# Delta-net inverses kept as two 64 x 64 diagonal blocks below the top level

## The reference

```
L = strict_lower((k * beta) @ k.T * decay);  a = L + I
sol = triangular_solve(a, [v * beta, k * beta * exp(gc)])
```

## Time and profile before

| | |
|---|---|
| median of 3 runs (lowest to highest) | 1391.28 us (1390.93 to 1394.15) |
| the profiled execution, its time | 1388.38 us |
| its span, 19281 instructions | 1386.8 us |
| PE busy | 1199.2 us (86%) |
| DVE, POOL, ACT busy | 579.5 (42%), 463.7 (33%), 382.1 (28%) us |
| mean granted TensorE clock | 0.942 of full speed |

### The profile page before, as it was taken

The page is one execution under the profiler, slowest core; times in us unless marked ns, Lnnn a source line. Parts: engine busy times, 40 slices in busy tenths (PEclk is TensorE's granted clock), DMA queues, the critical chain, the costliest instruction groups (busy, mean ns, idle before and its releaser), DMA issues. The chain is left out here.

```text
span 1386.8 us, 19281 instructions
## 1 busy us (share of the span) xinstructions
PE 1199.2 (86%) x7621; PEld 890.2 (64%) x7621; DVE 579.5 (42%) x1182; ACT 382.1 (28%) x796; POOL 463.7 (33%) x464
## 2 busy tenths in 40 slices
PE   5989999699998884999789999789999789998883
PEld 4866788655554442877678887678888745555541
DVE  4456863411111116454775455775474411111113
ACT  4325641011111003354333355333432111111000
POOL 1222001122222211155886166986230022222210
PEclk8999999699999996999999999999999789999997
DMA  7122035779999995021000111000327779999995
GB/s 222 62 67 77 1 124 211 308 290 387 380 390 393 382 378 216 3 82 39 2 1 1 62 61 61 1 1 1 152 78 270 308 285 372 386 391 385 387 369 212
DMA packets 65803, 270.29 MB, mean 195 GB/s; under 512 B 16812, under 2 KB 16908, under 8 KB 41136
## 3 DMA queue, kind: packets, MB, share of 16 engines
q1 hardware_dynamic: 54176, 247.50, 47.0%
q0 software_dynamic: 11392, 21.00, 4.5%
q10 hardware_dynamic: 144, 0.52, 0.1%
HBM read 262.69 MB, written 23.07 MB: 206 GB/s over the span
## 5 line engine op out<-in xcount | busy, mean ns | idle before, releaser
L874 POOL DMA_INDIRECT y_rows<-arena,idx_i x64 | 64.9, 1015 | 366.5 <-DVE arena L1153 359.6
L1489 PE MATMUL bank<-arena 128*128 128x128 f32 x1088 | 139.3, 284 | 17.2 <-DVE arena L2008 8.1
L1489 PEld LDWEIGHTS bank<-arena 128*128 128x128 f32 x1088 | 129.8, 196 | 29.9 <-DVE arena L2008 11.2
L991 PE MATMUL bank<-ring,arena 128*64 128x256 f32 x1024 | 126.2, 398 | 15.0 <-issue 14.0
L1157 DVE TENSOR_TENSOR arena<-arena,bank 128x128 f32<-128x128 f32 x64 | 18.4, 288 | 279.2 <-ACT arena L1068 279.2
L1068 ACT ACTIVATE arena<-bank 128x128 f32<-128x128 f32 x64 | 17.8, 278 | 379.6 <-PE bank L991 241.1
L144 PE MATMUL bank<-ring_r,ht_r 128*128 128x512 f32 x288 | 113.5, 394 | 0.0
L991 PEld LDWEIGHTS bank<-ring,arena 128*64 128x64 f32 x1024 | 76.2, 137 | 54.5 <-issue 16.9
L1153 DVE COPY arena<-bank 128x512 f32<-128x512 f32 x64 | 44.3, 692 | 149.4 <-PE bank L1000 149.4
L142 PE MATMUL bank<-ring_r,arena_r 128*128 128x512 f32 (+1 forms) x228 | 91.3, 400 | 5.4 <-DVE ring_r L166 3.4
L143 PE MATMUL bank<-ring_r,arena_r 128*128 128x512 f32 x224 | 88.3, 394 | 0.0
(11 more groups left out here) (303 smaller groups left out, 2364.3 us busy)
## 6 DMA issues: line engine op xcount, KB each, us to landing
ring<-in_moe_w_gate SPq DMA_DIRECT2D x32, 1024.0 KB
ring<-in_moe_w_up SPq DMA_DIRECT2D x32, 1024.0 KB
ring<-in_moe_w_down SPq DMA_DIRECT2D x26, 1024.0 KB
arena<-in_moe_w_down SPq DMA_DIRECT2D x20, 1024.0 KB
ring<-in_gdn_w_in SPq DMA_DIRECT2D x8, 2048.0 KB, 8.1
arena<-in_moe_w_gate SPq DMA_DIRECT2D x12, 1024.0 KB
arena<-in_moe_w_up SPq DMA_DIRECT2D x12, 1024.0 KB
spare<-in_moe_w_down SPq DMA_DIRECT2D x10, 1024.0 KB
```

Source lines behind the costliest of these rows:

```text
L874: pool.indirect_dma_start(out=y_rows[l], out_offset=bass.IndirectOffsetOnAxis(ap=idx_i[:, 1, e:e + 1], axis=0), in_=y_out[:, e % RING, :], ...
L991: last = pe.matmul(bank[1][m * SLOTS:(m + 1) * SLOTS, 0:2 * P].rearrange("p (w n) -> p w n", w=2), xgt[:, i, c * SLOTS:(c + 1) * SLOTS], w ...
L1489: last = pe.matmul(bank[b][:, h * P:(h + 1) * P], lhs(h), rhs(h), start=True, stop=True)
```

## The change

`level`, `seed` and a new `unit` become 128 x 64 masks: rows 0 to 63 hold the upper left block, rows 64 to 127 the lower right one. Up to level 5 (`TOP = 6`) the tiles `lm`, `w`, `r`, `s` and `st` hold only these two blocks, 4 heads x 64 columns, 256 in all. `sides_act` (ACT, two copies per chunk) cuts the blocks out of `lt`. Each product becomes two, one per block, on rows and columns 0 to 63 or 64 to 127 of the array; the turns become products with the identity. At level 6 `y` reads the two off-diagonal blocks of `lt` directly, and DVE writes the update into the off-diagonal blocks of `s` (two copies per slot). `make_v0`, `diag_pool` and `keep_pool` go: POOL keeps the masks `lm` and gets `top_pool` (two operations per slot, once per pair), ACT gets the copies by `move` and, at level 6, two copies per slot into the diagonal blocks of `s`.

```diff
+        def by_side(pe, b, lhs, rhs, across=False):
+            for h in range(HH):
+                for i, side in enumerate(SIDES):
+                    to = SIDES[1 - i] if across else side
+                    last = pe.matmul(bank[b][to, h * HB:(h + 1) * HB], lhs[side, h, to] if across else lhs[side, h, :],
+                                     rhs[side, h, :], start=True, stop=True)
+            return last
+        def turn_sides(pe, b, src):
+            for h in range(HH):
+                for side in SIDES:
+                    last = pe.matmul(bank[b][side, h * HB:(h + 1) * HB], src[side, h, :], ident[side, side],
+                                     start=True, stop=True)
...
-                    four(pe, 3 * slot, lambda h: lm[slot][:, h, :], lambda h: r_buf[l % 2][slot][:, h, :]
+                    by_side(pe, 3 * slot, lm[slot] if l < TOP else lt_of(2 * p + slot), r_buf[l % 2][slot],
+                            across=l == TOP).then_inc(g["y"], 1)
...
-                        turn_four(pe, 3 * slot + 2, s_buf[slot]).then_inc(g["t"], 1)
+                        turn_sides(pe, 3 * slot + 2, s_low[slot]).then_inc(g["t"], 1)
...
-                    four(pe, 3 * slot + 1, lambda h: st_buf[slot][:, h, :], lambda h: w_buf[slot][:, h, :]
+                    by_side(pe, 3 * slot + 1, st_low[slot], w_low[slot]).then_inc(g["un"], 1)
...
+        def sides_act(act, n):
+            act.wait_ge(g["lt"], n + 1)
+            for side in SIDES:
+                last = act.copy(lt_side_of(n)[side, :, :], lt_of(n)[side, :, side])
+            last.then_inc(g["lt_side"], 1)
...
+            if first:
+                for slot in range(2):
+                    sides_act(act, 2 * p + slot)
...
-                        act.copy(flat(st_buf[slot]), bank[3 * slot + 2][:, :]).then_inc(g["se"], 1)
+                        act.copy(flat(st_low[slot]), bank[3 * slot + 2][:, 0:HH * HB]).then_inc(g["se"], 1)
...
+                if l < TOP:
+                    for slot in range(2):
+                        act.activation(flat(s_low[slot]), flat(r_buf[l % 2][slot]), ACT.Copy,
+                                       scale=move[:, l:l + 1]).then_inc(g["rb"], 1)
+                else:
+                    for slot in range(2):
+                        act.wait_ge(g["top"], 2 * p + slot + 1)
+                        for side in SIDES:
+                            last = act.copy(s_buf[slot][side, :, side], lm[slot][side, :, :])
+                        last.then_inc(g["top_kept"], 1)
...
+        def top_pool(pool, o, p, slot):
+            pool.wait_ge(g["y"], at_level(p, TOP - 1, slot))
+            pool.wait_ge(g["r"], at_level(p, TOP, slot))
+            o.step(pool.tensor_tensor(lm[slot], r_buf[TOP % 2][slot], by_head_side(unit), ALU.subtract))
+            pool.wait_ge(g["sn"], at_level(p, TOP - 1, slot))
+            pool.tensor_tensor(lm[slot], lm[slot], s_low[slot], ALU.add).then_inc(g["top"], 1)
...
-                    pool.tensor_tensor(lm[slot], lt_of(n), by_head(level[l]), ALU.mult).then_inc(g["lm"], 1)
+                    pool.tensor_tensor(lm[slot], lt_side_of(n), by_head_side(level[l]), ALU.mult).then_inc(g["lm"], 1)
...
+        def first_st_r(dve, o, n, b):
+            dve.wait_ge(g["lt_side"], n + 1)
...
+            dve.tensor_tensor(st_low[n % 2], lt_side_of(n), by_head_side(seed), ALU.mult)
+            dve.wait_ge(g["m1"], n + 1)
+            o.step(dve.tensor_tensor(r_odd[n % 2], sides_in(bank[b]), by_head_side(seed), ALU.mult))
+            dve.tensor_tensor(st_low[n % 2], st_low[n % 2], by_head_side(unit), ALU.add)
+            dve.tensor_tensor(r_odd[n % 2], r_odd[n % 2], by_head_side(unit), ALU.add).then_inc(g["r"], 1)
...
+                        for i, side in enumerate(SIDES):
+                            last = dve.tensor_copy(s_buf[slot][side, :, SIDES[1 - i]],
+                                                   sides_in(bank[3 * slot + 1])[side, :, :])
+                        last.then_inc(g["sn"], 1)
```

More of the change, by code:

```diff
@@ L701, in build @@
         DIRS, LEVELS = 2, 7
-        MASKS = LEVELS + 4
+        TOP, HB = LEVELS - 1, P // 2
+        SIDES = (slice(0, HB), slice(HB, P))
+        MASKS = 7
         MASKS_AT = 17408 - MASKS * P
[L704 to L708, removed]
+        side_masks = cut(MASKS_AT, TOP + 2, HB)
+        level = [None] + [side_masks[:, l - 1, :] for l in range(1, TOP)]
+        seed, unit = side_masks[:, TOP - 1, :], side_masks[:, TOP, :]
+        incl = cut(MASKS_AT + 4 * P, DIRS, P)
+        below = cut(MASKS_AT + 6 * P, P)
         differ = cut(0, P)
-        at_least = cut(D, LEVELS + 1, P)
+        differ_s = cut(P, HB)
+        incl_s = cut(2 * P, DIRS, HB)
+        at_least = cut(D, TOP + 1, HB)
         bits = cut(2 * D, 2 * P).bitcast(I32).rearrange("p (w n) -> p w n", w=2)
         odd = cut(2 * D + 2 * P, LEVELS)
-        swap = cut(2 * D + 3 * P, P)
-        lower = cut(3 * D, LEVELS + 1, P)
+        swap = cut(2 * D + 3 * P, HB)
+        lower = cut(3 * D, TOP, HB)
         stay = sb("stay", [P, LEVELS])
@@ L736, in masks_dve @@
             o.step(dve.tensor_copy(differ, bits[:, 0, :]))
[L737 to L740, removed]
+            for side in SIDES:
+                dve.tensor_copy(differ_s[side, :], differ[side, side])
+                dve.tensor_copy(unit[side, :], ident[side, side])
+                for d in range(DIRS):
+                    dve.tensor_copy(incl_s[side, d, :], incl_of(d)[side, side])
@@ L741, in masks_dve @@
+            dve.memset(odd[SIDES[0], TOP:LEVELS], 0.0)
+            o.step(dve.memset(odd[SIDES[1], TOP:LEVELS], 1.0))
+            for l in range(TOP):
+                dve.tensor_scalar(at_least[:, l, :], differ_s, float(2 ** l), None, ALU.is_ge)
+            o.step(dve.memset(at_least[:, TOP, :], 0.0))
+            for l in range(1, TOP):
                 dve.tensor_tensor(level[l], at_least[:, l, :], at_least[:, l + 1, :], ALU.subtract)
             o.step(dve.tensor_tensor(seed, at_least[:, 1, :], at_least[:, 0, :], ALU.subtract))
-            for l in range(1, LEVELS):
-                dve.tensor_tensor(lower[:, l, :], level[l], incl_of(0), ALU.mult)
@@ L745, in masks_dve @@
[L745 to L748, removed]
+            for l in range(1, TOP):
+                dve.tensor_tensor(lower[:, l, :], level[l], incl_s[:, 0, :], ALU.mult)
+            dve.tensor_tensor(swap, incl_s[:, 1, :], incl_s[:, 0, :], ALU.subtract)
+            o.step(dve.tensor_tensor(below, incl_of(0), ident[:, :], ALU.subtract))
@@ L755, in masks_dve @@
-            o.step(dve.tensor_tensor(swap, swap, incl_of(0), ALU.add))
-            dve.tensor_tensor(inside, swap, at_least[:, 1, :], ALU.mult).then_inc(masks_made, 1)
+            dve.tensor_tensor(stay[:, 1:TOP], odd[:, 1:TOP], odd[:, 2:LEVELS], ALU.is_equal)
+            o.step(dve.tensor_scalar(swap, swap, odd[:, 1:2], None, ALU.mult))
+            dve.tensor_scalar(move[:, 1:TOP], stay[:, 1:TOP], -1.0, 1.0, ALU.mult, ALU.add)
+            o.step(dve.tensor_tensor(swap, swap, incl_s[:, 0, :], ALU.add))
@@ L1327, in by_head, with by_head_side @@
             return row.unsqueeze(1).to_broadcast([P, HH, P])
+        def by_head_side(row):
+            return row.unsqueeze(1).to_broadcast([P, HH, HB])
         def col(name, c, hf, d):
@@ L1804, in inverse_pool @@
                 select_pool(pool, 2 * p + 1)
-                diag_pool(pool, 2 * p)
-                diag_pool(pool, 2 * p + 1)
-            for l in range(1, LEVELS):
+            for l in range(1, TOP):
                 for slot in range(2):
@@ L1824, in inverse_pool @@
                     select_pool(pool, 2 * p + 3)
-                if first and l in (4, 6):
-                    diag_pool(pool, 2 * p + l // 2)
             for slot in range(2):
-                keep_pool(pool, p, LEVELS - 1, slot)
+                top_pool(pool, o, p, slot)
         def scan_pool(pool, hf, n):
```

125 lines of the change are left out of this document (53 added, 72 removed), and 1 row of the table g.

## The result

The changed kernel takes 1353.95 us (median of 4 runs, 1350.37 to 1357.97), the kernel before 1391.45 us beside it: ratio 0.9733, 95% interval 0.9716 to 0.9749. It is faster by 37.5 us; the forecast was 47 us, 1344. The profiled execution took 1353.42 us, 34.96 less than that of before, where 47.2 were forecast.

What follows compares the result with a forecast made beforehand. GpSimd was taken as the bound in the second pair, PE only 10% behind. Per half 12.0 + 12.6 + 1.0 - 2.0 = 23.6 us, 47.2 in all: 1341.2 profiled, 1344 median; own range 1334 to 1358, overall 1334 to 1390.

Steps and rivals of the forecast that it cites:

- The pace of a group, T: PE time for a group of 16 64 x 64 records, a head's two blocks side by side: 0.45 us, 0.50 with waits.
- The rule in the Trainium skill: Objection in the inverses' products: one bank forces a head's blocks to run serially, group 0.9 us, about 1391; chance 0.08.
- One level: One level of the inverses, through PE, ScalarE's copy and VectorE's new r: 3.4 us, against 5.56 before.
- GpSimd, ScalarE, VectorE off the path: Per level, GpSimd's masks take 1.5 us, ScalarE and VectorE 2.7 each; all fit into 3.4.
- Second pair: Second pair of chunks in each half's inverses: 23.5 us against 35.45, 12.0 saved.
- five such steps 17.0: Second pair's first five levels, all taken as equal at 3.4 us each, 17.0 together.
- rival (c): Slower inverses, by PE record cost or the lower clock throughout: 1404 us, about 1510 with both; chance 0.15.
- First pair: First pair of chunks in each half's inverses: 32.0 us against 44.6, 12.6 saved.
- The start of a half: Before level 1, `make_v0` and `diag_pool` leave the path and `sides_act` enters: 1.0 us saved, between 0 and 2.
- Changes of tile shape: Ten switches between PE tile shapes in each half, at 0.2 us each: 2.0 us lost.
- The two halves alike: Both halves of the heads counted as equal, 80.05 us of inverses each before, 23.6 saved in each.
- Everything else unmoved: Outside the inverses: savings pass on in full to everything behind, and the layer 0 mask changes count 0.

Runs made afterwards that it cites:

- m7_quads: Separate program, not the kernel, running only small fp32 products on PE by quadrant order and bank: 0.059 us a record in one quadrant, 0.030 on opposite quadrants in turn.
- e4_both: Changed kernel with `last_m` turns moved ahead of the next pair's level 1, and VectorE making both chunks' r before both st: 1346.09 us.
- e6_order: Changed kernel with one edit, VectorE makes both chunks' r before both chunks' st: 1345.63 us.
- e9_sides: e4_both plus `sides_act` of the first two chunks placed ahead of the third chunk's exponentials on ScalarE: 1341.60 us.

## Why the prediction was right, and by how much it was off

- **The pace of a group, T.** Forecast 0.45, taken as 0.50; measured 0.46 (32 records in 1.10). The step that decided was right, and m7_quads shows it by itself. The reason given with it, that the weight load sets the pace, was not tested.
- **The rule in the Trainium skill** (TensorEngine Tiling (Array Packing), Restrictions and Gotchas: different row tiles cannot access one PSUM bank at the same time) would have made it 1391. Measured: a head's two blocks, on different row tiles, write the same bank, and the group takes 2.08 us with one bank as with two. The measurement decides, for blocks that land on different partitions. Whether the rule holds where both land on the same partitions, no run here shows.
- **One level.** Forecast 3.4, measured 3.44, by the path that was forecast. From the first `y` (903.52) the first turn starts 0.98 later (forecast, with the measured T: 2T = 0.92), its copy on ScalarE 1.66 (3T + 0.22 = 1.60), the first update 2.18 (3T + 0.65 = 2.03), VectorE's new r 2.89 (4T + 0.87 = 2.71), the next `y` 3.43 (4T + 1.4 = 3.24). So hand-overs and seams cost 0.2 more than allowed. That 3.4 came out so closely is in part luck: T, taken 0.04 too high, made up for it.
- **GpSimd, ScalarE, VectorE off the path.** Right; GpSimd fell from 29.9 to 9.4 us in the second pair (12 forecast).
- **Second pair.** Forecast 23.5, measured 27.02. Its levels, between the first products of each, took 6.1, 3.9, 3.4, 3.4, 3.4 and 6.8 with the end; forecast five times 3.4 and 6.5. The failed step is the sentence "five such steps 17.0": the first of them also holds `last_m`, VectorE's order and, since PE had waited 2.3 us, the lower clock. I wrote that the clock would be near 1.00 from the first pair's level 2 on; it was 0.50 here. That is the fall of the clock of rival (c), but for some 6 us at a seam and not through the inverses.
- **First pair.** Forecast 32.0, measured 33.43. Level 1 took 8.05 for 5.9: the second chunk's first product came 2.75 us behind the first's. The other five took 5.6, 3.5, 6.3, 3.4 and 6.5, together 25.4 for 26.1.
- **The start of a half.** 1.0 forecast, 0.3 measured (the last `silu` to the first product went from 15.8 to 15.5 us): the copies and VectorE's four operations fill what `diag_pool` and `make_v0` left.
- **Changes of tile shape.** 0.2 each, 2.0 a half. In m7_quads the step into a group of 64 x 64 is 0.52 instead of 0.43 and the next one 0.10 instead of 0.05; out of it, 0.15 instead of 0.03 and then 0.53 instead of 0.43: 0.14 in, 0.22 out. The size was right.
- **The two halves alike.** Not so: 17.6 and 19.7 us were saved. The first half's level 1 and the start of its second pair ran longer at the lower clock.
- **A reading in rival (c).** "PE busy 84% and 89%" stands in the wrong order, and the clock of the first pair is 0.94 in the earlier trace rows, not 0.93: the first pair has 84%, the second 89%. No term of the sum rests on it.
- **Everything else unmoved.** 2.5 us were lost in layer 0, in work that the change does not touch. The first router products start at 241.76 before, and after at 244.24:

```profile
244.24 0.98 PE L355 MATMUL bank<-router,ht 128*128 128x36 f32 x8
```

The shift arises in two steps, at 25 to 30 us and at 75 to 88, where products begin behind a wait at the lower clock. A product of L142 to L144 takes 0.63 there and starts every 0.43; later it takes 0.39 and starts every 0.23. Before, 13 of them were slow in the two places, after, 25: 12 x 0.20 = 2.4 us. Before, the clock had risen at this point:

```profile
29.16 0.39 PE L142 MATMUL bank<-ring_r,arena_r 128*128 128x512 f32 x1
```

After, it had not:

```profile
29.10 0.63 PE L144 MATMUL bank<-ring_r,ht_r 128*128 128x512 f32 x1
```

This differs from execution to execution: e4_both, e6_order and e9_sides have the same code up to there as the changed kernel, and have 16, 25 and 25 slow ones and their first router products at 242.17, 244.31 and 244.22. The nine kernels with the change's masks lie between 242.0 and 244.3, the two without at 241.8 and 242.8; that the masks have a small part in it is not excluded.

The account, in us: forecast 47.2; less 6.0 in the first half, 3.9 in the second, 2.5 in layer 0; and 0.2 gained behind: 35.0, the difference of the profiled executions. With VectorE's order mended alone (e6), the kernel stands at 1345.6, 2 us from the forecast. That does not confirm the sum: the forecast had counted VectorE's operations in the old order and no time at the lower clock behind them.

## What to carry to other kernels

Small products that leave quadrants of the array free are worth packing: price them from rows of the same width, and let neighbours in the queue stand on different quadrants, because the order alone was worth about 18 us here. When a stage gets shorter, look at what PE waits for at its seams: here gaps of about 2 us were often followed by the lower clock, which cost 2.0 us a half, and filling one with products that nobody reads shortened the stage behind it (the gain in the whole time, 2.7 and 2.4 us by the medians, is within the intervals). And where a chain view puts a short "issue" between two groups of PE, look in the timeline and the code for a copy that ended just before.

## What was not expected of the hardware

- All four quadrants in turn run at 0.015 us a record, a quarter of one quadrant's 0.059; sharing rows or columns cost nothing (2.08 us a group in every kind of pair, with two banks where the columns are shared).
- Runs of four products (eight records) in one quadrant still overlap with the next quadrant's, 0.039 a record instead of 0.059.
- Behind a gap of 2.3 us the granted clock was 0.50 for some 6 us in the changed kernel, in both halves, though in the first half not at once; behind 1.7 in e6_order it stayed at 1.00. The length of the gap alone does not decide: behind 1.9 in e9_sides it fell in one half and stayed in the other. Adding 2.0 us of useless products in each half shortened the second pairs by 2.4 and 1.6 us.
- One of VectorE's additions over 256 columns took 1.25 us instead of 0.42 while GpSimd's product over 512 columns (L1830) ran beside it, at the start of a half:

```profile
858.23 0.69 DVE L2021 TENSOR_TENSOR arena<-arena 128x256 f32<-128x256 f32 x1
858.59 2.40 POOL L1830 TENSOR_TENSOR ring<-arena 128x512 f32<-128x512 f32 x2
858.84 1.25 DVE L2022 TENSOR_TENSOR arena<-arena 128x256 f32<-128x256 f32 x1
```
